# Order of four score matmuls and the waits ahead of the last input projections

## The reference

```
sh_a, sc_a, g_a, sh_f, sc_f, g_f = split(silu(c) @ w_ada + b_ada, 6)      # 1024 x 6144
hx = rmsnorm(x) * (1 + sc_a) + sh_a ;  hc = the same of ctx with c_ctx
px = hx @ w_in                                  # q, k, v for 4 heads, and the pooling part
kc, vc = hc @ w_in[:, 512:1536]                 # keys and values of the context
q, k = rope(q), rope(k)                         # two halves of 64 per head
s1 = q1 k1^T / 8 ; s2 = q2 k2^T / 8             # per head: 512 x 768
a = softmax(s1) - lam * softmax(s2) ;  att = rmsnorm(a v)
pool = centred window means of px's last 512 columns, mixed by w_pool
x = x + g_a * rmsnorm(concat(att, pool) @ w_out)
```

## Time and profile before

| | |
|---|---|
| median of 3 runs | 1020.88 us (1019.31 to 1021.87) |
| the profiled execution | 1021.87 us, of which its instructions span 1019.7 us |
| granted clock of PE, mean | 0.978 of full speed |
| PE busy | 947.9 us, 93% of the span |
| DVE, ACT, POOL busy | 519.2, 330.5, 391.6 us |
| moved by DMA | 298.04 MB |

### The profile page before, as it was taken

One profiled execution on the slowest core, in us unless ns is written; L12 is line 12 of the kernel. 1 busy time (PEld: TensorE's weight loads), 2 busy tenths in 40 slices (PEclk: granted clock), 3 DMA queues, 4 the chain that ended last, 5 costly groups with the idle time before them and its releaser, 6 DMA issues.

```text
span 1019.7 us, 13919 instructions
## 1 busy us (share of the span) xinstructions
PE 947.9 (93%) x4003; PEld 395.6 (39%) x4004; DVE 519.2 (51%) x697; ACT 330.5 (32%) x594; POOL 391.6 (38%) x298
## 2 busy tenths in 40 slices
PE   3899999999999989889999899996999999999696
PEld 1644444676455633223333233332333333333232
DVE  1346888785357835335454334443345455445245
ACT  4212221676345312223322232222223323322232
POOL 0313331000000064445565544555355565556520
PEclk9999999999999999999999899998999999999898
DMA  9955551630326849999989999999999999999946
GB/s 370 353 195 206 185 205 44 220 163 1 145 85 241 336 169 378 391 387 370 386 267 373 404 390 365 374 369 364 390 368 367 368 325 379 375 356 363 342 139 185
DMA packets 62669, 298.04 MB, mean 292 GB/s; under 512 B 14590, under 2 KB 15586, under 8 KB 34609
## 3 DMA queue, kind: packets, MB, share of 16 engines
q1 hardware_dynamic: 42850, 260.11, 64.4%
q0 software_dynamic: 18736, 35.41, 14.4%
q10 hardware_dynamic: 1056, 2.18, 0.6%
HBM read 282.15 MB, written 38.27 MB: 314 GB/s over the span
## 4 chain that ended last, share of the span: by engine, by line
DMA 45%; PE 44%; SPq 5%; DVE 3%; issue 2%; ACT 1%; ACTq 0%; POOL 0%; DVEq 0%; POOLq 0%
DMA wring<-in_w_e_down 39%; PE psum L993 12%; PE psum L1241 9%; PE psum L1253 4%; PE psum L1084 3%; DMA wring<-in_w_e_up 3%; PE psum L1064 3%; DMA heads<-in_w_ada 3%; PE psum L1055 2%; PE psum L1031 2%; SPq L473 2%; SPq L449 2%; PE psum L1203 2%; PE psum L969 1%; PE psum L1336 1%
## 5 line engine op out<-in xcount | busy, mean ns | idle before, releaser
L1241 PE MATMUL psum<-wring,xres 128*64 x832 | 381.1, 612 | 35.8 <-DVE cur_g L1695 33.3
L1241 PE MATMUL psum<-cur_g,xres 128*64 128x512 f32 x832 | 381.1, 612 | 0.0
L577 POOL DMA_INDIRECT xg<-h_rows,gidx x216 | 246.9, 1143 | 215.9 <-ACT gidx L830 142.1
L1241 PEld LDWEIGHTS psum<-wring,xres 128*64 128x64 f32 x832 | 112.7, 141 | 260.4 <-issue 255.6
L1699 DVE STREAM_TRANSPOSE xres<-xg 128x1024 f32<-128x1024 f32 x53 | 108.4, 2046 | 161.9 <-DMA xg<-h_rows,gidx 159.8
L1253 PE MATMUL psum<-wring,rows 128*64 x416 | 188.7, 597 | 1.9 <-ACT rows L826 1.9
L1253 PE MATMUL psum<-rows 128*64 128x512 f32 x416 | 188.8, 597 | 0.0
L1695 DVE COPY cur_g<-wring 128x1536 f32 x106 | 125.7, 1228 | 45.6 <-SPq L462 43.1
L584 POOL DMA_INDIRECT expert_sums<-xres,sidx x50 | 86.7, 1735 | 93.5 <-DMA expert_sums<-xres,sidx 82.4
L888 ACT COPY xres<-psum 128x1024 f32<-128x1024 f32 x52 | 52.6, 1012 | 193.9 <-PE psum L1253 99.0
L1241 PEld LDWEIGHTS psum<-cur_g,xres 128*64 128x64 f32 x832 | 112.7, 141 | 0.0
(11 more groups left out here) (259 smaller groups left out, 919.7 us busy)
## 6 DMA issues: line engine op xcount, KB each, us to landing
wring<-in_w_e_gate SPq DMA_DIRECT2D x64, 1024.0 KB
wring<-in_w_e_up SPq DMA_DIRECT2D x64, 1024.0 KB
wring<-in_w_e_down SPq DMA_DIRECT2D x64, 1024.0 KB
ring<-in_w_ada SPq DMA_DIRECT2D x20, 1024.0 KB, 4.7
ring<-in_w_in SPq DMA_DIRECT2D x3, 2048.0 KB, 25.8
heads<-in_w_ada SPq DMA_DIRECT2D x4, 1024.0 KB, 22.9
ring<-in_w_out SPq DMA_DIRECT2D x1, 4096.0 KB, 13.2
acc<-expert_sums SPq DMA_DIRECT2D x8, 512.0 KB, 6.3
```

The costliest lines, as they stand in the source:

```text
L577: pool.indirect_dma_start(xg[q][:, 256 * s:256 * s + 256], None, hrows, bass.IndirectOffsetOnAxis(gidx[:, q, s:s + 1].bitcast(U32), 0), bo ...
L1241: last = pe.matmul(pp[2][SUB * g:SUB * g + SUB, 512 * q:512 * q + 2 * F] .rearrange("p (u f) -> p u f", u=2), xT[:, q, k, SUB * g:SUB * g ...
```

## The change

Three edits, all in PE's list.

1. `project(n)`: tiles 18 and 19 had no wait for `s_ipe`. Now tile 18 waits for 17 (tile 16 copied) and tile 19 for 18 (tile 17 copied). The waits of all other tiles stay.
2. `modulation_rows(0)`: its first two matmuls no longer wait for `s_ipe` at 15 and 16.
3. `scores(u)`: the matmul of (s, c0) = (0, 0) with 512 columns is issued ahead of that of (1, 0) with 256, where it came behind it. The other two keep their places.

```diff
@@ project(n) @@
-                if n < 18:
-                    pe.wait_ge(s_ipe, n - 3)
-                elif n >= 20:
-                    pe.wait_ge(s_ipe, n - 1)
+                pe.wait_ge(s_ipe, n - 3 if n < 18 else n - 1)
@@ modulation_rows(half) @@
                     if half:
                         pe.wait_ge(s_adre, cc - 3)
-                    elif cc < 2:
-                        pe.wait_ge(s_ipe, 15 + cc)
@@ scores(u) @@
-                for s, c0, n in ((1, 0, 256), (0, 0, 512), (1, 256, 512), (0, 512, 256)):
+                for s, c0, n in ((0, 0, 512), (1, 0, 256), (1, 256, 512), (0, 512, 256)):
```

## The result

The changed kernel takes 1028.44 us (median of 6 runs, 1026.17 to 1032.77) where the kernel before takes 1020.85 (6 runs, 1019.31 to 1021.87): 7.6 us slower by the medians. Over all its 24 runs (median 1026.61) the ratio is 1.0063, with a 95% interval of 1.0044 to 1.0083, so between 4.5 and 8.5 us; the six runs lie at the high end of that. The forecast of 1022.0 with a range up to 1024.9 was too low. The profiled execution has a span of 1023.5 us, 3.8 more than that of before, so a single pair of profiles doesn't show the whole loss. The stages show it better.

A forecast was written before the change was run, and what follows sets the result against it. Neither engine bounds the kernel everywhere; PE, without slack, bounds projection through scores. Stall +1.16, removed waits 0, score order 0: +1.16 us on the median 1020.88 gives 1022.0 us, range 1019.5 to 1024.9.

The forecast's parts named there:

- What bounds the stage: Projection tiles to scores: PE has no slack, so delays carry on; in the attention loop, extra score time counts once per unit.
- Tile 18's wait and edit 2: Projection and rows of ones: tile 16 copied 3.0 us before needed, removed waits met 17 us before; cost and gain nothing.
- Tile 19's wait: Between tiles 18 and 19: copy of tile 17 1.00 us late, plus restart, a 1.16 us stall carried to the end.
- The bound of 2.1 us: Upper limit of the stall ahead of tile 19, from waits before line 688 differing by up to 0.44 us; lower limit 0.
- Edit 3, costed at 0 with bounds of 0.2 us: Attention scores: the new order only exchanges which half starts first by 0.01 us; 0, within 0.2 us over 16 units.
- The cover that the forecast counted on: In a scores unit: release of the waiting matmul at 0.75 us, needed only at 0.97, hidden by the other half's work.
- three signs of being wrong: First s = 1 record 0.4 us behind; no gap ahead of tile 19; or a gap with the expert stage's start unmoved.
- the scores of a unit still 1.50 us: Expected in the changed profile's attention loop: first score record to next work unchanged at 1.50 us.
- The 3.4 us that the forecast worked out by the page: Scores under the skill's strict program order: 0.215 us more per unit, 3.4 in all, time 1025.5 us; rejected from the trace.
- The list's order binds the score matmuls: Rival, 5%: in scores the 256-column call cannot pass the 512-column call's two passes; 0.43 us per unit, 6.9 in all, 1028.9.
- No stall: Rival, 10%: half rows arrive earlier, or ACT is otherwise ahead by 1.16 us, so tile 19 is not delayed; 1020.9 us.
- The clock: Rival, 3%: three half-rate PE pieces in the expert stage vanish, -5.4 us, or -4.2 with the stall; 1016.7 us.

The follow-up runs named there:

- e1: Kernel before with only the changed `s_ipe` waits (tiles 18, 19 and rows of ones), score order old: 1021.95 us against 1019.64, ratio 1.0023.
- e2: Kernel before with only the score matmul order changed, (0, 0) ahead of (1, 0), old waits: 1025.91 us, ratio 1.0064.
- e7: Kernel before with the wait for the copy of tile 17 put ahead of tile 18, old score order: 1028.55 us against 1019.11, ratio 1.0098.
- e5: Kernel before with the changed `s_ipe` waits, old score order, and the last `w_ada` half row scaled behind ACT's copy of tile 17: ratio 1.0013.
- e3: Kernel before with both score calls of s = 1 listed ahead of both of s = 0, old waits: ratio 0.9997.
- e6: Kernel before with s = 0 first, its 512-column call cut into two of 256, only one ahead of (1, 0), old waits: ratio 0.9994.
- e9: Kernel before with the halves exchanged: (1,256), (0,512), (0,0), (1,0), where the (1,0) call waits for the end of (0,512): ratio 1.0041.
- e8: Changed kernel with the last `w_ada` half row scaled behind ACT's copy of tile 17: 1024.94 us against 1019.49, ratio 1.0056.

## Why the prediction was wrong

**What bounds the stage: right.** A stall ahead of tile 19 and a longer unit both reach the end. The totals of e1 (+2.3 us), e2 (+6.5) and e7 (+10.0) show it, within their intervals.

**Tile 18's wait and edit 2, costed at nothing: right.** In e5, which has both, PE has no gap.

**Tile 19's wait, +1.16 us: right in kind, mis-sized.** The term was read from one execution, as the distance between two things that don't depend on each other: when the tiles began (50.47) and when the last half row came (151.99). With this wait, the gap is the lag less 100.36 by the forecast's own working: 101.52 gives the forecast's 1.16, 101.99 gives 1.63 (1.62 measured in e1), and 103.77 gives 3.41 (3.40 measured after). The eleven lags in the table, taken the same way, would give 0 to 3.8 us, with a mean of 2.0. The execution of before had the third smallest lag. The bound of 2.1 us came from the spread of the single waits before line 688 and left out that the tiles' own start moves too, by up to 3.5 us among the eleven executions (49.42 to 52.90). That the term is 2 and not 1.16 moves the forecast by 1 us; alone it would have stayed in the range.

**Edit 3, costed at 0 with bounds of 0.2 us: wrong, and this is the step that failed.** The text says that the (1, 0) call "has streamed at 0.11 + 2 x 0.215 = 0.54 us after the unit's start, a record ends 0.16 later (0.59 - 0.43), and the release takes 0.05: 0.75". It took the moment of the release from the call's own end. In the kernel before that call was first in the list, so its own end and its turn to report were the same, and the 0.75 of that trace could not tell them apart. In the changed kernel the 512-column call is ahead and ends at 1.12, the semaphore is raised at 1.15, and the waiting load starts at 1.195. The cover that the forecast counted on, up to 0.97, is gone. The term is 0.33 us for a unit and 5.34 for the loop. None of the three signs of being wrong that the forecast named came up (the first record of s = 1 is 0.007 us behind, there is a gap, the expert stage moved); none of them looks at the release. What failed in kind was its "the scores of a unit still 1.50 us": they took 1.82.

The forecast had looked for a rule about order and asked only whether starts follow it. The Trainium skill, in "TensorE: Matmul & The Clock Gate", Part 3 ("The mechanism"), says that both starts and ends follow the order of the program. For the starts this kernel disagrees (the second call's first record is 0.007 us behind the first call's first and ahead of its second, in both kernels; in e3 it is 0.013 behind and ahead of three). For the ends, as a semaphore sees them, it agrees (0.03 us behind the long call's end, after). The trace had disproved the half of the sentence that could be seen, and the whole was put aside. The 3.4 us that the forecast worked out by the page is not what happened either: it counted in starts that wait in turn.

**The rivals.** "The list's order binds the score matmuls" gave 1028.9, near the 1028.44 measured, but by another mechanism. It said it would decide if the first record of s = 1 started over 0.2 us behind, with 6.9 us for the loop. That record started 0.007 us behind, and the loop lost 5.34; e3 speaks against that mechanism directly. Its time came near by luck: its 6.9 is 1.6 too large for the loop and its stall of 1.16 about 0.8 too small, and the median of six runs lies above that of all 24, 1026.61. "No stall" held in neither profile with the wait of tile 19 and the old place of the scaling (after and e1), but it can happen: the lags of e6 and e9, 100.03 and 100.60, would leave a stall of 0 and 0.2 us. "The clock": the first expert pass of the profiled execution after did start at full clock, and the last two columns of the table differ by 3.1 and 6.4 us among executions, but not by edit as far as can be seen.

**The sum as it turned out:** about 2 us for the wait and 5.34 for the order, 7.3, against 7.6 by the medians of six runs and 4.5 to 8.5, with 6.4 in the middle, by the ratio over all.

## What to carry to other kernels

When matmuls on different halves of PE overlap, put the call whose end somebody waits for ahead of longer calls in the list: wherever a call of the other half was listed ahead here, the report came behind that call's end, even where this was 0.4 us later than its own. That it waits for more than the one call ahead was not tried. A margin between two chains that don't wait for each other (here PE's tiles and ACT's half rows) is a quantity with a spread, and one profile gives one draw of it; before costing a new wait between them, read both start times in as many executions as there are. And where a rule has two halves, test each one against the trace.

## What the runs showed of the hardware

- Matmuls of two halves of PE's rows start out of list order (three records passed, 0.013 us apart, e3), but a semaphore on the shorter one is raised 0.03 us behind the modelled end of the longer one listed ahead of it (at 1.15 us of the unit, where its own end is 0.70: after, e2, e8, e9), and the weight load that waits for it starts 0.04 us later.
- A matmul whose weight load waits for such a release loses more than the later start: the load was 0.44 us later (0.75 to 1.195) and the unit 0.33, of which 0.23 is the later start of the last call (0.970 to 1.197) and 0.11 the longer distance to its second pass (0.320 behind the first, where it was 0.215), the same 0.11 as at any first weight load of a unit.
- Behind 9.05 us in which PE was idle, the granted clock was 0.50 (1.2 GHz) for another 4.9 us (155.18 to 160.07, e7). Behind the 3.14 us of the changed kernel it was 1.00 and nothing was slower: tile 19 takes 6.97 us from 155.78 to the rows of ones at 162.75, which is 6.87 and the first weight load's 0.11.
